# Where the fourth part of a top-k selection stands among the steps of an attention round

## The reference, cut to what matters

```python
def block(args):
    qb, qib, wb, pb = args
    score = jnp.einsum('bqhd,bsd->bqhs', qib, k_idx).astype(jnp.float32) * IDX_DIM ** -0.5
    index = jnp.einsum('bqhs,bqh->bqs', jax.nn.relu(score), wb.astype(jnp.float32)) * IDX_HEADS ** -0.5
    index = jnp.where(allowed[None], index, -jnp.inf)
    top_val, top_idx = lax.top_k(index, n_sel)      # n_sel = 256
    ks = gather(k, top_idx)
    vs = gather(v, top_idx)
    s = jnp.einsum('bqkgd,bqskd->bqkgs', qg, ks).astype(jnp.float32) * HEAD_DIM ** -0.5
    ...
    p = jax.nn.softmax(s, axis=-1)
    o = jnp.einsum('bqkgs,bqskd->bqkgd', p.astype(v.dtype), vs)
```

## Time and profile before

| | |
|---|---|
| median of 3 runs | 4156.05 us (4155.38 to 4160.89) |
| the profiled execution | 4160.89 us, its span 4159.1 us |
| busy in the span | PE 3545.4 us (85%), DVE 2033.9 (49%), ACT 894.4 (22%), POOL 109.8 (3%) |
| 2190 to 2950 us, where the changed rounds are | 760 us: PE 555.22, DVE 637.82, ACT 309.09 us busy; mean granted clock of PE 0.79 |
| MAX8, L2340 | 224 of them, 246.2 us |
| MATCH_REPLACE8, L2345 | 224 of them, 243.1 us |
| maximum, L2186, waits for first scores, L2079 | 70.5 us in 33 waits |

### The profile page before, as it was taken

The page is one execution under the profiler, slowest core; times in us unless marked ns, Lnnn a source line. Parts: engine busy times, 40 slices in busy tenths (PEclk is TensorE's granted clock), DMA queues, the critical chain, the costliest instruction groups (busy, mean ns, idle before and its releaser), DMA issues. The chain is left out here.

```text
span 4159.1 us, 61088 instructions
## 1 busy us (share of the span) xinstructions
PE 3545.4 (85%) x26584; PEld 3221.4 (77%) x26603; DVE 2033.9 (49%) x2978; ACT 894.4 (22%) x1664; POOL 109.8 (3%) x51
## 2 busy tenths in 40 slices
PE   7978589878999999989977777776556899999996
PEld 6977279767999999979954445454434899999996
DVE  4415866446323223452127888898565542323235
ACT  1006411112101001120034444443223120101011
POOL 0010000001000000100000000000000100000001
PEclk9988599988999999989976788887677999999998
DMA  3110000111111111122210000001110111111111
GB/s 98 46 41 22 5 5 4 49 36 31 46 42 45 46 41 46 36 84 68 68 60 1 1 1 1 1 1 31 51 31 26 36 41 41 46 42 45 47 41 48
DMA packets 245728, 151.04 MB, mean 36 GB/s; under 512 B 33701, under 2 KB 239930, under 8 KB 244698
## 3 DMA queue, kind: packets, MB, share of 16 engines
q1 hardware_dynamic: 244504, 146.92, 11.9%
q10 hardware_dynamic: 962, 0.20, 0.0%
HBM read 127.08 MB, written 19.79 MB: 35 GB/s over the span
## 5 line engine op out<-in xcount | busy, mean ns | idle before, releaser
L239 PE MATMUL psum<-rounded,rounded 128*128 128x364 f32 x13464 | 2272.1, 330 | 66.4 <-DVE rounded L320 30.9
L239 PEld LDWEIGHTS psum<-rounded,rounded 128*128 128x128 f32 x13464 | 2256.2, 189 | 76.6 <-issue 64.5
L786 ACT ACTIVATE arena<-psum 128x1092 f32<-128x1092 f32 x64 | 69.4, 1084 | 1194.4 <-PE psum L239 1194.4
L800 DVE CAST rounded<-arena 128x1092 fp32r<-128x1092 f32 x64 | 46.7, 730 | 529.5 <-ACT arena L789 529.5
L225 DVE TENSOR_TENSOR rounded<-arena,rounded 128x1024 fp32r<-128x1024 f32 x187 | 276.7, 1479 | 6.5
L1554 PE MATMUL psum<-arena 64*64 64x64 f32 x8160 | 256.8, 220 | 23.9 <-POOL arena L1738 12.5
L2114 PE MATMUL psum<-arena 128*128 128x128 f32 (+2 forms) x1424 | 241.3, 324 | 41.7 <-ACT arena L2178 41.6
L1554 PEld LDWEIGHTS psum<-arena 64*64 64x64 f32 x8160 | 246.2, 136 | 35.4 <-DVE arena L1691 18.4
L2114 PEld LDWEIGHTS psum<-arena 128*128 128x128 f32 (+1 forms) x1424 | 217.1, 232 | 67.3 <-issue 40.4
L2098 PE MATMUL psum<-arena 128*128 128x128 f32 (+1 forms) x712 | 142.3, 337 | 134.7 <-ACT arena L2169 134.2
L2340 DVE MAX8 arena<-arena 128x8 f32<-128x384 f32 (+6 forms) x224 | 246.2, 1099 | 4.0
(11 more groups left out here) (231 smaller groups left out, 2594.5 us busy)
## 6 DMA issues: line engine op xcount, KB each, us to landing
arena<-in_w_ff_up SPq DMA_DIRECT2D x128, 256.0 KB, 3.2
arena<-in_w_ff_down SPq DMA_DIRECT2D x128, 256.0 KB, 3.0
arena<-in_w_in_odd SPq DMA_DIRECT2D x44, 256.0 KB, 3.2
arena<-in_w_in_even SPq DMA_DIRECT2D x40, 256.0 KB, 3.5
x_kept<-arena SPq DMA_DIRECT2D x2, 4368.0 KB, 12.5
arena<-x_kept SPq DMA_DIRECT2D x2, 4368.0 KB, 13.3
arena<-in_x_prompt SPq DMA_DIRECT2D x1, 4096.0 KB, 19.5
arena<-in_cache_c_k SPq DMA_DIRECT2D x4, 1024.0 KB, 5.6
```

The costliest lines, as they stand in the source:

```text
L239: last = nc.tensor.matmul(m.ps[:, out:out + TB], rounded(m, w)[:, k, :], rounded(m, x(k))[:, b * TB:(b + 1) * TB], start=(k == 0 and n == ...
```

## The change

In the prompt rounds the early steps are `steps[:-1]`, that is three of four, before; they are `steps[:2]`, two of four, after. The late ones are the rest: one before, two after. The same instructions are issued on every engine; only their order on DVE differs. In the sample's rounds no step is early, before and after.

```diff
                     steps = range(EACH if t.topk else 0)
-                    early = steps[:-1] if len(t.f.units) > 1 else steps[:0]
+                    early = steps[:2] if len(t.f.units) > 1 else steps[:0]
                     for h in t.f.units[1:]:
                         maximum(dve, t, i, h)
                     select(dve, t.topk, t.done, i, early)
                     if after:
                         maximum(dve, *after, 0)
                     normalise(dve, t, i)
                     select(dve, t.topk, t.done, i, steps[len(early):])
```

## The result

The changed kernel takes 4241.2 us (median of 6 runs, 4236.04 to 4244.14), against 4156.03 us before (6 runs, 4152.51 to 4161.92). The ratio is 1.0199, with a 95% interval of 1.0188 to 1.0210: 85 us slower. The forecast was 4201, with a range up to 4224. The sign and the place were right, the size was half of what came.

The account below looks back on a forecast made before the run. DVE was taken to bound the rounds. Middle rounds 45.2 + last rounds 11.5 - run ends 8.9 - run with 2112 values 2.9 = 44.9 us, added to 4156: 4201 us, range 4172 to 4224.

Parts of the forecast that it names:

- DVE bounds the rounds, and only its idle time counts: Inside a round DVE's instructions are a fixed sum; a round gets longer only by what DVE idles.
- The length of a step: On DVE, a step (S) takes 1.25 to 2.58 us for 384 to 1024 values, 4.85 us for 2112.
- the slow round's price: Middle round at half clock: the wait for scores grows by a whole step, 1.8 us at 640 values.
- The fast round's price: Middle round at full clock: costs 0.33 to 0.60 us by run size, 15.2 us over all middle rounds.
- The middle rounds, 45.2 us: The 36 middle rounds cost 45.2 us in longer DVE waits, including 6.9 us at the normalisation.
- the last rounds' late step, 11.5 us: In each run's last round two late steps delay the maximum of unit 1 by one step: 11.5 us over six runs.
- R: Time from the start of unit 1's exponentials to the end of the first unit's scores: 3.55 or 5.45 us at 640 values.
- Bounds of the clock, +15 to +69 us: PE's unknown clock in middle rounds: total +15 us if all ran like the fast one, +69 if like the slow one.
- Run ends, -8.9 us: Last normalisation comes one step earlier and the values are in time: five runs gain 8.9 us, the sixth nothing.
- The run with 2112 values, -2.9 us: Late steps cost 3 x 4.85 us; early ones and the earlier last normalisation give back more: -2.9 us.
- my signs of being wrong: L2186 not waiting longer, the scores' time changed at equal clock, or time going outside 2200 to 2950 us.
- The rival "the half clock prevails": Longer PE waits throttle the clock; all 36 middle rounds cost a whole step: 4225 us, chance 0.08.

Follow-up runs that it names:

- both kernels filled: Unused extra matmuls put in PE's waits: changed kernel, in front of unit 1, 4179.5 us; kernel before, in front of both units, 4167.6 us.
- the half of the change alone: Kernel before with two early and two late steps only in the last round of each run: 4139.0 us, ratio 0.9950.

## Why the prediction was wrong, step by step

- *DVE bounds the rounds, and only its idle time counts.* Right. Its busy time stayed and the added waits make the added time.
- *The length of a step, and the slow round's price.* Right: a slow round cost 1.79 us at 640 values as worked out from the earlier trace rows.
- *The fast round's price.* About right: with both kernels filled, the order costs 26.3 us within the six runs, where the full-clock bound had 15.2 + 11.5 = 26.7. The whole kernel lost less (5.9 to 10 us against +15), since the run ends and the run with 2112 values gave back more than their terms.
- *The middle rounds, 45.2 us, and the last rounds' late step, 11.5 us.* This step failed. They came to 75.8 us instead of 56.7: the longer waits for scores to 60.2 us in the middle rounds (about 38 forecast) and 6.3 in the first rounds (11.5), those for values to 10.5 (6.9). The formula took R from the trace of before, round by round. With R as the trace of after shows it, in the same 36 rounds, its part without the values gives 58.9 us, where R of before gives 36.5; so the formula holds and its input was wrong. R depends on the granted clock (with 640 values 3.56 us at 1.00 and 5.46 at 0.50), and the clock fell where the change made PE wait longer: the wait in front of unit 1 grows, and the scores stand right behind it. The sentence that failed is "The rounds read now lie between, and I keep them as they are."
- *Bounds of the clock, +15 to +69 us.* The upper one was too low. It priced a half-clock round at S. Where R rises from under 3S to over it, a round costs more. The last middle round of the run with 896 values is such a one: R went from 4.38 to 7.16 us (3S is 6.96), DVE waits 2.79 us for the scores where it waited for nothing, and the round grew from 12.75 to 16.03 us, by 3.28 where S is 2.32; some 0.5 us of that is the wait for the values. The bound also left the values and the run ends at the old clock.
- *Run ends, -8.9 us.* Right by mechanism (the half of the change alone gives all of it and more) but undone in the changed kernel, where the ends came to +2.2 us. The waits at L2316 in five ends fell by 8.9 us, as forecast. What the term put at nothing was the rest: "the values are done in time" failed (6.0 us of waits in these ends), and the sixth end, forecast as neutral, grew by 2.4 us.
- *The run with 2112 values, -2.9 us.* Came to -1.4. The wait at its end fell from 9.10 to 5.73 us instead of to about 4.3; the other terms weren't taken apart.
- *The waits to be seen after.* I forecast about 120 us at L2186 where 141 came (70.5 before, whole kernel), +8 us for the values where 19 came, and -9 us at L2316 where -7.8 came. R at equal clock is what it was, and the time did go where it was forecast, so none of my signs of being wrong pointed at the fault: I had named none for the share of slow rounds.
- *The rival "the half clock prevails".* It came nearest, at a chance of 0.08: 28 of 36 rounds, and 4241 us against its 4225. The Trainium skill, "TensorE: Matmul & The Clock Gate", section "HAM oscillation — how this bites in real kernels", named the direction: waits between bursts of matmuls can throttle the array again. This case's traces agree: 28 of 36 rounds at half clock after the wait grew, none when it was filled in front of unit 1. I had cited the rule and kept the shares of the rows all the same, without asking which work of PE would stand right behind the wait that grows.

Not settled: which of PE's waits, or how much idle time in all, brings the half clock. The wait in front of unit 1 alone does not order the kernels: it adds up to 27 us in the kernel before with a mean clock of 0.71, to 37 us in the changed kernel filled there with 0.97, and to nothing with all steps early and 0.72. Nor are the 12 us behind the attention in two of the filled kernels explained.

## What to carry to other kernels

A duration on PE that is read at a certain clock is not safe in a sum that moves PE's waits: ask which PE work stands behind the wait that grows, and price it at half clock too, as a bound. Read the granted clock over that work, not over the stage. When one edit has two places with opposite signs, try them apart: here the smaller half alone was a gain of 0.5%.

## What the runs showed of the hardware

- The granted clock was 1.00 through a 3.3 us wait of PE (2575.40 to 2578.70) and 0.54 over the scores right after it. With the wait cut to 1.33 us by unused matmuls, the eight L2070 behind it took 1.56 us instead of 2.87, and the granted clock over the scores was 1.00.
- With no wait of PE in front of unit 1 at all (four early steps), 14 of 36 rounds still had their scores at half clock.
- Twenty matmuls of 128x256 in f16 took 2.35 us, and 864 matmuls of this shape, added to a kernel, made it 62 us faster than it was without them.
- Over the run with 768 values the mean granted clock was 0.83 and 0.82 before and after, while it fell from 0.79 to 0.62 over the work that mattered.
